# Asking for the next layer's weight panels at an earlier signal, and waiting behind a branch

## What is computed

```
for i in range(DEPTH):
    mp = adaln(c_ctx, w_ada[i], b_ada[i]);  ms = adaln(c, w_ada[i], b_ada[i])
    hp = modulate(rmsnorm(xp, norm1[i]), mp[0], mp[1])      # hs likewise
    yp, ys = mixer[i % 3](hp, hs)                          # attention, pool, retention
    xp = xp + mp[2] * yp;  xs = xs + ms[2] * ys
    hp = modulate(rmsnorm(xp, norm2[i]), mp[3], mp[4])
    xp = xp + mp[5] * moe(hp, ...);  xs = xs + ms[5] * moe(hs, ...)
y = rmsnorm(x, norm_f)
# moe: top-1 group, top-2 experts in it; act = silu(t@w_gate) * (t@w_up) * gate; y = act @ w_down
```

## Time and profile before

| | |
|---|---|
| median of 3 runs | 1492.85 us (1492.22 to 1496.95) |
| profiled execution | 1492.69 us |
| its span, first to last instruction | 1490.7 us |
| mean granted clock of TensorE | 0.981 |
| busy share of the span | PE 93%, DVE 49%, ACT 21%, POOL 6% |
| DMA | 417.70 MB, mean 280 GB/s |

### The profile page before, as it was taken

The page is one execution under the profiler, slowest core; times in us unless marked ns, Lnnn a source line. Parts: engine busy times, 40 slices in busy tenths (PEclk is TensorE's granted clock), DMA queues, the critical chain, the costliest instruction groups (busy, mean ns, idle before and its releaser), DMA issues. The chain is left out here.

```text
span 1490.7 us, 18178 instructions
## 1 busy us (share of the span) xinstructions
PE 1393.5 (93%) x6741; PEld 745.5 (50%) x6741; DVE 729.1 (49%) x1865; ACT 309.1 (21%) x697; POOL 92.0 (6%) x102
## 2 busy tenths in 40 slices
PE   6998998999799999899999999999997999999995
PEld 3335535444365443456666666446442446455442
DVE  1154304644426545566666666216542656155543
ACT  2104404111143111511111111013100306141011
POOL 0000011000220001000000000000000110110003
PEclk9999999999899999999999999999999999999998
DMA  9979967899778997645555555247999931039995
GB/s 381 406 317 360 421 271 287 343 423 400 277 286 332 423 422 271 243 132 170 178 183 183 170 167 198 102 180 296 413 423 388 374 128 64 29 142 362 423 423 218
DMA packets 122613, 417.70 MB, mean 280 GB/s; under 512 B 7232, under 2 KB 63392, under 8 KB 86560
## 3 DMA queue, kind: packets, MB, share of 16 engines
q1 hardware_dynamic: 107152, 378.07, 65.2%
q10 hardware_dynamic: 11920, 25.94, 4.6%
q0 software_dynamic: 3456, 12.58, 2.4%
HBM read 395.04 MB, written 21.53 MB: 279 GB/s over the span
## 5 line engine op out<-in xcount | busy, mean ns | idle before, releaser
L1232 PE MATMUL bank<-gate_up_weights,hT_gathered 128*64 128x512 f32 (+1 forms) x1280 | 257.4, 605 | 14.7 <-SPq L583 14.7
L1043 PE MATMUL bank<-panel,hT 128*128 128x512 f32 x384 | 169.3, 601 | 4.6 <-DMA panel<-in_ret_w_in 3.7
L1232 PEld LDWEIGHTS bank<-gate_up_weights,hT_gathered 128*64 128x64 f32 (+1 forms) x1280 | 82.1, 134 | 182.1 <-issue 181.7
L1246 PE MATMUL bank<-down_weights,actT 128*64 128x512 f32 (+1 forms) x640 | 131.5, 598 | 4.6 <-ACT actT L2622 4.6
L1043 PEld LDWEIGHTS bank<-panel,hT 128*128 128x128 f32 x384 | 73.9, 193 | 94.8 <-issue 89.3
L1762 DVE SCALAR_TENSOR_TENSOR ada_sums<-panel,cond_columns,ada_sums 128x384 f32<-128x384 f32 x224 | 121.1, 610 | 0.0
L1217 PE MATMUL bank<-P,h_hi 128*128 128x256 f32 x384 | 99.5, 296 | 3.8 <-DVE P L2041 3.8
L2610 ACT ACTIVATE silu<-bank 128x256 f32<-128x256 f32 x36 | 13.8, 383 | 390.7 <-PE bank L1232 390.7
L1217 PE MATMUL bank<-P,h_lo 128*128 128x256 f32 x384 | 94.2, 283 | 0.0
L1217 PEld LDWEIGHTS bank<-P,h_hi 128*128 128x128 f32 x384 | 73.3, 191 | 26.8 <-issue 19.5
L697 PE MATMUL bank<-panel,oT 128*128 128x512 f32 x192 | 84.3, 595 | 1.3 <-ACT oT L2501 0.7
(11 more groups left out here) (406 smaller groups left out, 1882.8 us busy)
## 6 DMA issues: line engine op xcount, KB each, us to landing
gate_up_weights<-in_gate_up_halves SPq DMA_DIRECT2D x136, 1024.0 KB, 13.6
down_weights<-in_down_rows SPq DMA_DIRECT2D x68, 1024.0 KB, 14.5
panel<-in_ada_panels SPq DMA_DIRECT2D x54, 1024.0 KB
panel<-in_w_ada SPq DMA_DIRECT2D x16, 1536.0 KB
ada_panel_third<-in_ada_panels SPq DMA_DIRECT2D x18, 1024.0 KB
y_by_slot<-y_rows ACTq DMA_DIRECT2D x32, 512.0 KB, 7.9
panel<-in_ret_w_in SPq DMA_DIRECT2D x16, 1024.0 KB
panel<-in_attn_w_qkv SPq DMA_DIRECT2D x5, 2048.0 KB
```

The lines of the kernel that those rows point to most:

```text
L1043: last = PE.matmul(ps[t][:], hT[:, k, t * 128:(t + 1) * 128], panel[f % 2][:, k, :], start=k == 0, stop=k == KD - 1)
L1232: last = PE.matmul(ps[2][width * s:width * s + width, :], hT_of(k)[:, width * s:width * s + width], gu_ring[w][:, 2 * k // KD, :, k % (KD ...
L1246: last = PE.matmul(ps[6 + half][width * s:width * s + width, :], actT[:, c, width * s:width * s + width], dn_ring[w][:, c, half * 512:half ...
```

## The change

The wait for `row_gateup` stays. The wait for `quads_done` moves behind a branch on the number of extra passes of the layer just ended, which SP has in a register.

```diff
             n = first_panel["end", l] - f
             if l:
                 sp.wait_ge(sem("row_gateup"), ROWS * l)
-                sp.wait_ge(sem("quads_done"), l)
+                with sp.If(passes[l - 1] > 0):
+                    sp.wait_ge(sem("quads_done"), l)
                 if l % 3 == 2:
```

## The result

The changed kernel takes 1497.3 us, median of 20 runs (1493.9 to 1500.1); the kernel before, on the same chips, 1492.5 (20 runs). The ratio is 1.0026, with a 95% interval of 1.0019 to 1.0034: 3.9 us slower, 2.8 to 5.1. The profiled execution has a span of 1496.8 us, 6.1 more than before.

What follows compares the result with a forecast made beforehand. PE's waits at layer changes were taken as limiting: DVE's tile behind gather 3, a retention panel, then `hT`. Terms 3.25 - 0.4 - 1.5 = +1.35 us on 1492.69 gave 1494.0; own range 1490.5 to 1497, widened to 1488.0 to 1499.2.

Steps and rivals of the forecast that it cites:

- The forecast's own range: Whole kernel: 1490.5 to 1497 us, said to come from the terms' bounds taken one at a time.
- The branch, 0.2 us: SyncE at each change of layer: the new branch takes 0.2 us, so requests move ahead by 3.25 and 3.1 us.
- The rival in which it eats the advance: SyncE's new branch costs some 4.4 us, second request 1.1 us later than now; 1492.7 us, chance 0.11.
- First change, +3.25: First change of layer: panels slow the gathers from 290 to 145 GB/s for 3.25 us; pool matrix starts 3.25 us later.
- The upper bound of +4.8: First change: all 1.39 MB of gathers that ran alone shared from the start, at 145 instead of 290 GB/s.
- sign of about 10 us of idle time: First change: PE's idle time ahead of the pool matrix would be about 10 us instead of 6.84.
- Second change, -0.4: Second change: PE starts the retention's products 0.4 us earlier through better use of the DMA engines; bounds 0.4 and 2.9.
- the order of the two inputs: Second change: gather 3 1.7 us late, `hT` ready at 600.4, still ahead of the panel at 601.4.
- Clock behind it, -1.5: Behind the second change: PE's idle stretch is broken in two, saving half the 3.0 us clock cost; bounds 0 and -3.0.
- Third change, 0: Third change: gather 3 at most 1.8 us later, within 3.2 us of cover ahead of DVE's add; no loss.
- the early request is all gain: Rival: gathers keep their rate, panel comes 3.1 us earlier; second change -2.9, clock -3.0; 1486.8 us, chance 0.11.
- The gathers pay for all of it: Rival: first change +4.8 and +1.7 for longer low clock, second change 0; together +6.5, 1499.2 us, chance 0.16.

Runs made afterwards that it cites:

- measured alone: Kernel before with the branch and early request at that one change of layer only: first change 1499.2 us (1.0044), third change 1493.0 us (1.0004).
- six traces that ask as before: Traces of the kernel before and five experiment kernels with the second change's request unmoved; scatter to products 12.6 to 14.1 us, first 16 products 8.56 to 9.97.
- all behind gather 3: Kernel before with the first change's panels asked for only when gather 3 has landed, other changes as before; 1488.2 us, ratio 0.9974.
- second change alone: Kernel before with the branch and early request at the second change of layer only; 1490.1 us, ratio 0.9981.
- first change alone: Kernel before with the branch and early request at the first change of layer only; 1499.2 us, ratio 1.0044.

## Why the prediction was right, and where its sizes were off

The result of +3.9 us (2.8 to 5.1) lies in the range, above the +1.35 of the forecast. It is within the 0.3% that the forecast called no change, but twenty runs of each kernel tell it from nothing: it is a small slowdown. The mechanism was right: a loss at the first change, a smaller gain at the second, little at the third. Two terms were mis-sized, the first and the third change, both towards too small a loss. The forecast's own range is also wider than its working: bounds taken one at a time end at 1495.8, and its 1497 takes two of them together. On the profiled execution +3.9 is 1496.6, above the first and below the second.

- **The branch, 0.2 us.** Right: 0.15 at all three changes (384.44 to 384.59, 588.79 to 588.94, 1157.27 to 1157.42). The rival in which it eats the advance is out. The Trainium skill, in Runtime: NRT & Kernel Launch, section Instruction fetch mechanics, has a taken branch wait for a fetch when its target is outside the stretch already held. The 0.15 us show no such wait, with a target one instruction on.
- **First change, +3.25.** The mechanism was right, the size too small: 5.7 us in the two traces, 6.6 measured alone. The step that failed is the one that gives the gathers back only what they lose in 3.25 us at half rate. It took the 290 GB/s of the earlier trace rows as all that they can move alone, so that panels beside them seemed to cost less than their full time: by its own rates, 1.8 MB more of them for 3.25 us. Left alone behind a jam the gathers moved 402. So every MB of panels ahead costs its full time, 2.28 us, and there were 2.4 MB more of them: 5.5 us, and measured on gather 3 it is 6.2 (15.7 against 9.5). The upper bound of +4.8 rested on the same rate, and was broken too. Nor did the sign of about 10 us of idle time ahead of the pool matrix come (5.59), since the wait moved ahead of the scatter. That the clock behind the pool matrix would be as low as before was right (0.57, and 7.06 us for the products as before).
- **Second change, -0.4.** The 0.35 and 0.48 us of the traces agree with it by luck. The step that failed is the order of the two inputs: `hT` was to be ready 1 us ahead of the panel, and it comes last, because gather 3 takes 2.6 us longer (9.4 against 6.8) and not 1.7. The panel lands some 0.9 us earlier, more than the 0.4, but the products start within the spread of the six traces that ask as before. That most of the 3.1 us would be paid back by the gathers is supported from the other side: 4.0 us later cost 1.3.
- **Clock behind it, -1.5.** Nearer than the two traces say. They have -2.87, nearly the bound of -3.0, but the 9.97 us from which both are counted are those of one execution; from the 8.56 to 8.83 of the other five it is -1.5 to -1.7. The idle stretch was broken up as foreseen, and the clock did not fall at all. The gaps were 2.37 and 0.88 us and not 1.6 and 1.7, since tile 0 was turned 2.5 us late instead of 1.7.
- **Third change, 0.** +1.3 and +1.7 us in two traces, +0.6 measured alone. The step that failed is the start of SyncE's packets. Put 2.75 us behind the request, they were to meet only the end of gather 3 and make it at most 1.8 us late, beside 3.2 us of cover. They came 1.1 us behind it, ahead of the gather's own, and gather 3 was 4.5 us late (8.8 instead of 4.3).

Of the rivals, "the early request is all gain" fell at the first change. The Trainium skill, in DMA: Bandwidth & Descriptors, section Rules for kernel authors, advises to issue a transfer early. Here that is borne out where the transfer is waited for (0.9981 at the second change, if through the clock) and reversed where it is not: at the first change early costs 1.0044 and late gives 0.9974. "The gathers pay for all of it" had +6.5, near the first change's 6.6 by luck: 1.7 of it was a longer stretch at the low clock, which did not come, and it missed the gain at the second.

What stays open is why the gathers get next to nothing for some 2 us when SyncE's transfers set in. It is so with long and with short packets, and at the third change for 3.3 us. At the first change it costs nothing of its own.

## What to carry to other kernels

Ask at each request who waits for it and whose transfer it goes ahead of: a weight panel that nobody misses, asked for 3.3 us earlier, held back by 6 us a small transfer that the path waited for; asked for 6 us later, it made the kernel 3.9 us faster. Count the bytes that are served ahead of the awaited transfer; the rate that it has when it is alone is no measure of what it could have. And look at the clock behind a wait before the wait itself is attacked: 16 more idle matmuls got most of what the earlier panel got.

## What the hardware showed beyond what was expected

- **The last of 16 parts sets a landing.** The trace has 16 landing events for each gather. Of gather 3 at the first change, in us of the span:

```
                                  issue    first    8th      last
before                            386.70   395.23   395.47   396.22
changed kernel                    387.44   400.72   401.07   403.12
all behind gather 3               388.21   392.71   393.40   394.03
```

  In the changed kernel the last part comes 2.1 us behind the 8th, before 0.75. So of the 6.2 us by which the landing is later 4.9 are in the 8th part too, and 1.3 are in the last one.
- **Onset.** From 388 to 389 us SyncE's queue had all that moved (0.43 MB) in the changed kernel, and gather 1, issued at 384.95, nothing.
- **Idle gaps and the clock.** A gap of 2.37 us at the second change left the granted clock at 1.00 in the changed kernel, and one of 2.24 in the second change alone; in the kernel before a gap of 2.05 us in layer 1 was followed by 0.56, and with the first change alone one of 2.19 ahead of the retention's products by 8.83 us for these, not 7.10. The length of the last gap alone does not tell.
